# Wide steps of an attention kernel: transposes of both key blocks ahead of the value products of both

## The reference

```python
s = jnp.einsum('bthc,bmhc->bhtm', q, k).astype(jnp.float32) * (q.shape[-1] ** -0.5)
p = jax.nn.softmax(s, axis=-1)
return jnp.einsum('bhtm,bmhc->bthc', p.astype(v.dtype), v)
...
o = o * jax.nn.silu(gate)
x = x + o @ w_out[layer]
```

## Time and profile before

| | us |
|---|---|
| median of 3 runs | 758.38 (754.58 to 758.91) |
| profiled execution, whole | 759.62 |
| its span in the trace | 757.8 |
| its mean granted clock of PE, as a share of full speed | 0.97 |

### The profile page before, as it was taken

How to read it: one execution, slowest core, us unless ns; L and a number is a source line. 1 busy time by engine, 2 the same in 40 slices (tenths; PEclk the granted TensorE clock), 3 DMA queues, 4 the chain that set the end, 5 groups by cost and what they waited for, 6 DMA issues and landing times.

```text
span 757.8 us, 11465 instructions
## 1 busy us (share of the span) xinstructions
PE 693.6 (92%) x4229; PEld 546.2 (72%) x4229; DVE 435.2 (57%) x1004; ACT 333.5 (44%) x634; POOL 131.2 (17%) x94
## 2 busy tenths in 40 slices
PE   2999999889999999999999999998979966999995
PEld 2777787657777777777777777776766744778884
DVE  3946764464663595559755975597634456222433
ACT  5775654353353363426342534363535447131411
POOL 2021110110311311131113101411140024011320
PEclk9999999899999999999999999999989988899998
DMA  8421102101111221211121112111121027114331
GB/s 293 123 74 28 29 29 57 28 15 29 42 51 40 79 56 42 84 42 29 43 84 43 29 42 85 42 30 42 29 70 34 11 85 247 34 31 153 108 110 55
DMA packets 53175, 48.76 MB, mean 64 GB/s; under 512 B 5744, under 2 KB 45696, under 8 KB 53120
## 3 DMA queue, kind: packets, MB, share of 16 engines
q1 hardware_dynamic: 53120, 48.02, 20.5%
HBM read 40.15 MB, written 7.86 MB: 63 GB/s over the span
## 4 chain that ended last, share of the span: by engine, by line
PE 79%; DVE 7%; issue 3%; ACT 3%; DMA 3%; POOL 1%; SPq 1%; DVEq 0%; ACTq 0%; POOLq 0%
PE j_ps L1287 24%; PE s_ps L1287 10%; PE o_ps L1422 8%; PE pt_ps L1398 8%; PE j_ps L1469 6%; PE s_ps L1469 6%; PE s_ps L1323 5%; PE o_ps L1287 3%; PE s_ps L1342 3%; PE pt_ps L1342 2%; DVE picked L1052 2%; DMA bias<-in_w_out_dram 1%; PE pt_ps L1444 1%; PE j_ps L1263 1%; PE o_ps L1263 1%
## 5 line engine op out<-in xcount | busy, mean ns | idle before, releaser
L1287 PE MATMUL j_ps<-h_hi,w_hl 128*128 128x512 f32 (+2 forms) x624 | 204.0, 392 | 2.0 <-DVE h_lo L932 1.1
L1287 PEld LDWEIGHTS j_ps<-h_hi,w_hl 128*128 128x128 f32 (+1 forms) x624 | 116.1, 187 | 26.1 <-issue 2.8
L588 POOL TENSOR_TENSOR w_hl<-w_raw,w_hl 128x1024 fp32r<-128x1024 f32 (+1 forms) x29 | 68.1, 2347 | 347.5 <-ACT w_hl L685 335.1
L1287 PE MATMUL j_ps<-h_lo,w_hl 128*128 128x512 f32 (+2 forms) x312 | 119.7, 384 | 0.0
L832 ACT ACTIVATE probT<-pt_ps 128x512 f32<-128x512 f32 (+3 forms) x88 | 41.3, 469 | 153.5 <-PE pt_ps L1398 152.9
L844 ACT ACTIVATE prob<-prob,nmax 128x256 f32<-128x256 f32 (+7 forms) x128 | 89.8, 703 | 40.9 <-DVE nmax L1126 36.9
L1398 PE MATMUL pt_ps<-ident,prob 128*128 128x128 f32 x496 | 77.3, 292 | 7.3 <-DVE gate L1153 6.6
L1287 PE MATMUL s_ps<-h_hi,w_hl 128*128 128x512 f32 x240 | 81.6, 410 | 1.0 <-POOL w_hl L588 1.0
L1398 PEld LDWEIGHTS pt_ps<-ident,prob 128*128 128x128 f32 x496 | 55.8, 146 | 28.5 <-issue 24.6
L1052 DVE TENSOR_SCALAR_CACHE_REDUCE picked<-idx,tk 128x384 f32<-128x384 f32 (+5 forms) x72 | 67.9, 943 | 1.5
L1287 PEld LDWEIGHTS j_ps<-h_lo,w_hl 128*128 128x128 f32 (+1 forms) x312 | 58.6, 188 | 10.6
(11 more groups left out here) (217 smaller groups left out, 1070.1 us busy)
## 6 DMA issues: line engine op xcount, KB each, us to landing
w_raw<-in_w_in_dram SPq DMA_DIRECT2D x27, 512.0 KB, 3.8
bias<-in_a_tab_dram SPq DMA_DIRECT2D x8, 512.0 KB, 5.2
mixed_scratch<-gate SPq DMA_DIRECT2D x14, 256.0 KB, 2.3
bias<-mixed_scratch SPq DMA_DIRECT2D x8, 448.0 KB, 5.2
bias<-in_w_out_dram SPq DMA_DIRECT2D x6, 512.0 KB, 3.7
idx<-in_x_dram SPq DMA_DIRECT2D x4, 512.0 KB, 5.5
probT<-in_w_mem_kv_dram SPq DMA_DIRECT2D x4, 512.0 KB, 6.6
prob<-in_x_dram SPq DMA_DIRECT2D x4, 512.0 KB, 4.5
```

Source lines behind the costliest of these rows:

```text
L588: pool.tensor_tensor(w_hl[:, w % 2, 1, :, 0:n], raw_of(w)[:, :, 0:n], w_hl[:, w % 2, 0, :, 0:n].bitcast(F32), ALU.subtract).then_inc(w_lo_ ...
L1287: last = pe.matmul(bank[0:n, at:], a[:, k, 0:n], c[:, k, HALF * b + at:HALF * b + HALF], start=(k == 0 and q == 0), stop=(k == KD - 1 and ...
```

## The change

The order in which PE issues the work of one step is changed; every call stays, with the same arguments. In a wide step the second chunk's transposes and the second half of the projection (or the second early half of the output projection) come ahead of the first chunk's value products, which are then followed directly by the second chunk's.

```diff
                 if early[0]:
                     project_out(*early[0])
-                if s >= 1:
-                    values(s - 1, 0)
                 if two:
                     turn_prob(s - 1, 1)
-                if early[1]:
-                    project_out(*early[1])
                 if s < STEPS and projection_of_step(s):
                     if two:
                         fill(m, range(KD // 2, KD))
                     m += 1
+                if early[1]:
+                    project_out(*early[1])
+                if s >= 1:
+                    values(s - 1, 0)
                 if two:
                     values(s - 1, 1)
```

## The result

| | before | after |
|---|---|---|
| median, us | 755.47 (754.00 to 758.91, 6 runs) | 747.03 (742.61 to 751.83, 6 runs) |
| ratio | | 0.9885, 95% interval 0.9839 to 0.9931 |
| profiled execution, whole | 759.62 | 751.83 |
| its span | 757.8 | 750.0 |

The kernel became 1.15% faster, some 8.7 us; on record stood 7.2 us (751.2, "within 1%" the likeliest). In a second comparison, beside three other kernels on one chip (run e5), the ratio was 0.9878 (0.9845 to 0.9911). So the direction was that of the sum, the size was short, and the side of the 1% bound was missed. The granted clock was not the difference: its median over the executions is 0.974 to 0.976 for the kernel before (three sets, 51 executions) and 0.974 and 0.9755 for the changed one (two sets, 12). One more execution of the kernel before, of 1140 us at a granted clock of 0.56, is left out here and in the ratio.

What follows compares the result with a forecast made beforehand. PE was taken as the bound, busy 92% of the span. Projection steps -5.1, the three steps with nothing else -2.75 and the end +0.65 gave -7.2 us from the median 758.4: 751.2 us, range 747 to 756.

Steps and rivals of the forecast that it cites:

- The 17 projection steps: Wide steps with a projection on PE: one entry into and one exit from a value group saved, 0.30 us each, 5.1 less.
- the free join: In projection steps, the two chunks' value products follow without a gap; a full entry or exit would cost 0.15 us.
- That wait only changes its owner: The second transposes wait for the first chunk's copies at the point where the first value products had; nothing later.
- steps 48 and 56: Steps with nothing else to issue: first value products lie over the second copies' wait; 0.95 and 1.04 us less.
- Step 53: A step with nothing else to issue and one tile in its second chunk: 2.30 us becomes 1.54, 0.76 less.
- The end: Steps 61 to 64, with output projection halves: 0.65 us more together, bounds -0.3 and 1.7.
- (a): Rival: only the waits are won, switches between kinds of matmul cost the same anywhere; -1.2 us, 757.2 us; chance 0.12.
- (b): Rival: DVE makes PE wait in pair 5, losing the gains of 12 earlier projection steps, 3.6 us; 754.8 us; chance 0.03.
- (c): Rival: PE's clock improves, sparing the slow stretch from 643.8 us, the groups at 551.62, or both; 746.7 to 749.6; chance 0.18.
- (d): Rival: PE's clock falls more often, about 1.6 us each; one to four more leave 752.8 to 757.6 us; chance 0.09.
- A sign that came: On PE's clock: the prediction is wrong if the stretches at 0.5 of the clock differ by more than one.

Runs made afterwards that it cites:

- e5: The changed kernel run again with no edit, for a second trace and its time beside other kernels on one chip: 746.86 us, ratio 0.9878.
- e6: The changed kernel with the projection's second half put between the two chunks' value products: 753.46 us, ratio 0.9960.
- e4: The changed kernel with one more wait, so the second chunk's transposes start only when both heads' copies are done: 745.58 us, ratio 0.9844.
- e1: The kernel before, with the new order only in the 17 steps with a projection: 750.07 us, ratio 0.9896.
- e2: The kernel before, with the new order only in steps 48, 53 and 56: 751.57 us, ratio 0.9950.
- e7: The changed kernel, but in steps 61 to 64 the first chunk's value products come ahead of the second early output half: 744.62 us, ratio 0.9839.
- e3: The kernel before, with the new order only in steps 61 to 64: 758.75 us, ratio 1.0012.
- e8: The kernel before run again with no edit, for a second trace: 755.47 us, ratio 0.9982.

## Why the prediction was right or wrong, point by point

- **What bounds the kernel: right.** It is PE's chain: DVE's and ACT's busy time moved by 1.1 us and less, and each piece taken off PE in these steps shortened the step by as much.
- **The 17 projection steps: right**, 5.28 us for 5.1. Every part held: 0.23 from projection to transposes, no gap in the joined value group, the free join taken over the upper bound of 0.15. e6 shows it from the other side. The Trainium skill (TensorEngine Tiling (Array Packing), Key Properties) says that a change of tiling mode drains the engine and a change of tile alone does not; the traces agree, with 0.30 us for each value group spared and nothing at the join.
- **"That wait only changes its owner": wrong, the step that failed.** The wait of 1.63 us in steps 48 and 56 was carried over at its full length; measured were 0.30 us in both. Two things shorten it.
- **The smaller one is inside the step.** It was said that the second transposes wait for the same copies, at the same point, as the first value products had. But values waits for both heads ahead of its first matmul, turn_prob for one after the other, as its loop over a in the listing shows; so the transposes of head 0 went ahead under DVE's late copy. This was worth 0.37 us in step 56 and 0.14 in step 57, and next to nothing in 48 and 53 (e4).
- **The larger one comes from the step before: seen and not priced.** The prediction has "the evacuation of the projection, about 1 us earlier", and yet its working of s = 56 lets the transposes start at 612.33, behind the whole old wait. e1 prices it: 0.76 us in step 56 and, at equal clock, the same in step 48 (2.37 - 1.61). So step 56 was 2.24 for 1.04: 0.76, 0.37 and the 0.08 of waiting that the forecast had left. Step 48, at equal clock 3.51 - 1.61 = 1.9 for 0.95, lacked the same term of 0.76; there a wait of 0.20 us stayed ahead of the last value products, where "gone or under 0.1" was on record.
- **Step 53: right**, 0.78 for 0.76: no projection runs in step 52, so the term that was missed is not there.
- **Step 57: not seen.** 0.14 us shorter at equal clock. DVE's last piece in it (L1202, 2.98 us before, 2.84 after) ended 1.09 us behind POOL's (L635) in the traces of before, after and e2, and POOL's follows ACT's copy of step 56. The ten traces agree on this chain. Against the start of step 57, ACT's last copy of step 56 ends 0.14 us sooner than before in after, e5 and e7, 0.39 in e2 and e6, and not at all in e1, e3, e4 and e8; POOL's first piece starts and L1202 ends sooner by the same 0.14 and 0.39 (to 0.01), or not at all.
- **The end: right in sign, 0.4 for 0.65.** The new wait on DVE's add of the residual stands in step 62 of PE's timeline after:

```profile
653.41 0.60 PE L1398 MATMUL pt_ps<-ident,prob 128*128 128x128 f32 x4
654.35 0.50 PE L1469 MATMUL j_ps<-h_hi,w_hl 128*128 128x512 f32 x1 [0.35 <-DVE gate L1165]
```

  From start to start the four transposes take 0.94 where 0.36 would do, so the wait is 0.58 against the 0.67 on record, and the 0.35 in the bracket counts only from the modelled end. In steps 63 and 64, read the same way, it is 0.37 and 0.15 against 0.45 and 0.23. In step 61 the release came 0.73 us sooner (4.64 us from the first transposes to the output half where it was 5.37), for 0.67.
- **The rivals.** (a), waits alone, is ruled out by e1 and e6. (b), DVE gives it back, did not come: nothing was lost around step 45. (c), a better clock: it came in steps 48 and 61, but e8 has it with the old order, and over all executions the median granted clock is the same for both kernels, so it is not the 8.7 us. (d), more falls of the clock: steps 48, 53 and 56, the ones with adjacent transposes, were granted the full clock (1.00) in all six traces with the new order in them. (Its count was off by one: nine falls of 1.6 give 14.4 us, so ten, and not nine, would reach the 14.8 of "over 1% slower".) The Trainium skill (TensorE: Matmul & The Clock Gate, Part 4) says that transposes don't count as busy in the same way; the loss of 1.6 us a step worked out for that case did not show itself in these steps.
- **A sign that came, though the mechanism held.** The prediction called itself wrong if the stretches at the low clock differ by more than one. They do: against the first trace of before, step 48 has lost one and step 61 has a shorter one, while the prologue and step 18 have each gained one. But the two traces of before differ in steps 48 and 61 just so, so it was no good sign of being wrong.
- **The sum.** At equal clock the step lengths add up to -5.28 - 1.9 - 0.78 - 2.24 - 0.14 + 0.4 = -9.9 us, against 8.7 measured, within its interval (3.5 us on either side). The 1.4 us of the prologue, if they are the changed kernel's, would leave 8.5; the runs can't tell the two sums apart. On record stood 7.2. The missing 2.7 are 0.95 and 1.2 in steps 48 and 56, 0.14 in 57, 0.25 at the end, 0.2 elsewhere. With the bound at 7.6 us, that was the difference between "within 1%" and "faster"; as the forecast lay 0.4 us from the bound, it was also a matter of luck on which side it fell.

## What to carry to other kernels

When a group of instructions takes another's place behind a wait, compare the two waits semaphore by semaphore; one that is taken head by head lets half the work go ahead. When a step's work ends sooner, follow that queue into the next step before a wait there is carried over as it stands: this was the larger miss here. And on PE count how often unlike matmuls meet: this doesn't show in the busy share, and seventeen steps of 0.3 us were more than half of the gain.

## What the runs showed of the hardware

A group of value products in 64-column halves, between matmuls and transposes over the full width, cost 0.14 us to enter and 0.16 to leave, 0.30 in all. The single starts of step 21 before show where it lies: 0.32 us to its first matmul where 0.23 is the pitch, 0.15 to its second pair where the others take 0.10, 0.20 from its last matmul to the following transpose in place of 0.10, and 0.17 from that to the next transpose in place of 0.11. Projection matmuls and full-width transposes followed each other without such a gap (0.23 and 0.03 us from start to start). A wait that was already met cost nothing: the pitch of 0.11 us ran on between the heads' transposes and between the two value chunks. One and the same program ran step 48 in 9.43 us in one execution (granted clock 0.82) and in 7.82 in another (1.00).

On DVE a value read into a register, checked and branched on (L1088, L1089, L1096) held back the next copy until 1.0 us after the read began (549.78 to 550.79 in step 48 of the trace after), none of it counted as busy. And DVE's L1202, 1.23 us long by itself, took 2.59 to 2.98 us where it began while POOL worked on its L635, and ended 1.08 or 1.09 us after that in all ten traces. DVE's and POOL's timelines before, step 57:

```profile
618.45 2.98 DVE L1202 TENSOR_TENSOR h_lo<-bias,h_hi 128x1024 fp32r<-128x1024 f32 x1
...
623.88 1.23 DVE L1202 TENSOR_TENSOR h_lo<-bias,h_hi 128x1024 fp32r<-128x1024 f32 x1 [1.56 <-ACT h_hi L872]
...
618.01 2.33 POOL L635 TENSOR_TENSOR h_lo<-w_raw,h_hi 128x1024 fp32r<-128x1024 f32 x1
```
